# A decoder step on one core: a new order for the mixing stage, the output projection in eight pieces

## The reference, cut to what matters

```
u = rmsnorm(x, norm_mix) @ w_in                    # split into the head groups
m = concat(swa(q, k, v, sinks), gated_deltanet(conv(c), z, a, b, S0, ...))
h = x + m @ w_out
hn = rmsnorm(h, norm_ffn)
y = h + hierarchical_moe(hn, w_router_group, w_router_expert, ...)   # top 1 group, top 2 experts in it
out = rmsnorm(y, norm_final)
# gated delta rule, block by block, state S carried along:
#   v_new = u - w @ S;  o = q_dec @ S + qk @ v_new;  S = S * g_tot + k_dec.T @ v_new
# where u, w come from the inverse of (I + strictly lower (k k^T * beta * decay))
```

## Time and profile before

| | |
|---|---|
| median of 3 runs | 2366.58 us (2365.85 to 2373.49) |
| the profiled execution | 2381.16 us, its span 2379.3 us |
| mean granted clock of PE over the span | 0.949 |
| PE busy | 2218.0 us, 93% |
| DVE / ACT / POOL busy | 1276.8 / 543.3 / 641.1 us |
| positions start at | 0: 753.84, 1: 794.73, 2: 839.91, 5: 976.00, 6: 1047.45, 8: 1137.52, 11: 1280.29, 14: 1421.98, 15: 1471.21, 16: 1523.81 us |

### The profile page before, as it was taken

How to read it: one execution, slowest core, us unless ns; L and a number is a source line. 1 busy time by engine, 2 the same in 40 slices (tenths; PEclk the granted TensorE clock), 3 DMA queues, 4 the chain that set the end, 5 groups by cost and what they waited for, 6 DMA issues and landing times. The chain is left out here.

```text
span 2379.3 us, 47036 instructions
## 1 busy us (share of the span) xinstructions
PE 2218.0 (93%) x18536; PEld 1208.7 (51%) x18536; DVE 1276.8 (54%) x2659; ACT 543.3 (23%) x1417; POOL 641.1 (27%) x819
## 2 busy tenths in 40 slices
PE   7999999999976999899999999857999999999977
PEld 4454454454444666666666666633444444444433
DVE  4514325232424565355665746436776677667746
ACT  3202103112112343233434333310000000000013
POOL 1020100100200110211132231315655555555552
PEclk9999999999986899889999989977999999999998
DMA  8041040130168031112311221137999999999957
GB/s 310 18 136 47 24 142 23 47 112 13 35 180 219 6 118 53 51 57 87 108 62 62 97 87 62 44 146 276 351 366 366 367 374 367 376 377 372 351 224 311
DMA packets 171951, 405.87 MB, mean 171 GB/s; under 512 B 51187, under 2 KB 92771, under 8 KB 147161
## 3 DMA queue, kind: packets, MB, share of 16 engines
q1 hardware_dynamic: 142423, 350.39, 41.3%
q0 software_dynamic: 23648, 35.19, 4.1%
q10 hardware_dynamic: 5698, 17.67, 1.9%
HBM read 344.98 MB, written 94.80 MB: 185 GB/s over the span
## 5 line engine op out<-in xcount | busy, mean ns | idle before, releaser
L876 PE MATMUL p_ps<-p_xt,p_w 128*128 128x512 f32 x1088 | 474.1, 594 | 0.5 <-DVE p_xt L697 0.5
L3075 PE MATMUL p_ps<-p_w_arena,p_x_arena 128*128 128x512 f32 x1024 | 452.4, 595 | 11.1 <-DVE p_x_arena L2977 11.1
L876 PEld LDWEIGHTS p_ps<-p_xt,p_w 128*128 128x128 f32 x1088 | 204.1, 190 | 253.7 <-issue 248.5
L3075 PEld LDWEIGHTS p_ps<-p_w_arena,p_x_arena 128*128 128x128 f32 x1024 | 195.4, 191 | 257.4 <-issue 246.1
L2731 POOL DMA_INDIRECT p_x_arena<-s_hn,p_slot x272 | 276.8, 1018 | 122.2 <-issue 85.7
L2371 PE MATMUL p_ps<-p_w_out,p_mixt 128*128 128x512 f32 x544 | 258.5, 620 | 0.2 <-DVE p_mixt L1977 0.2
L2999 DVE STREAM_TRANSPOSE p_y_arena<-p_y_arena 32x64 f32<-32x64 f32 x1024 | 241.0, 235 | 13.2
L3084 PE MATMUL p_ps<-p_w_arena,p_y_arena 128*128 128x512 f32 x512 | 230.2, 592 | 3.2 <-DVE p_y_arena L2999 3.2
L3084 PEld LDWEIGHTS p_ps<-p_w_arena,p_y_arena 128*128 128x128 f32 x512 | 97.2, 190 | 126.0 <-issue 126.0
L2371 PEld LDWEIGHTS p_ps<-p_w_out,p_mixt 128*128 128x128 f32 x544 | 101.7, 197 | 107.6 <-issue 104.3
L885 PE MATMUL p_ps<-p_w,p_xt 128*128 128x144 f32 (+1 forms) x512 | 146.6, 439 | 0.0
(11 more groups left out here) (419 smaller groups left out, 2852.1 us busy)
## 6 DMA issues: line engine op xcount, KB each, us to landing
p_w_arena<-in_w_exp_gate SPq DMA_DIRECT2D x64, 1024.0 KB
p_w_arena<-in_w_exp_up SPq DMA_DIRECT2D x64, 1024.0 KB
p_w_arena<-in_w_exp_down SPq DMA_DIRECT2D x64, 1024.0 KB
p_w_arena<-s_y SPq DMA_DIRECT2D x16, 1024.0 KB, 14.7
p_x<-in_x_prompt SPq DMA_DIRECT2D x30, 512.0 KB, 4.8
p_w<-in_w_in SPq DMA_DIRECT2D x4, 2048.0 KB
p_spread<-s_roots SPq DMA_DIRECT2D x16, 512.0 KB, 7.0
s_kv<-p_us SPq DMA_DIRECT2D x32, 256.0 KB
```

The source lines that it names most:

```text
L876: ins = mm(ps[:, job % 4, :], w[:, c, at:at + P], xt[s % 2][:, c, :], start=(c == 0), stop=(c == KC - 1))
L3075: t = mm(ps[:, 2 + b, :], xt[b][:, c, :], w_gu[bw][:, :, c, :], start=(c == 0), stop=(c == KC - 1))
```

## The change

- PE's `project` takes pieces of two chunks. Eight pieces are spread over the whole position t for tile t - 1, the last at its end; so `layer_sum(t - 2, 1)` comes first in the next position, and `layer_norm`, `turn_hn` and `logits` follow in position t for tile t - 2. `mixt` and `h` become two buffers each.
- `pair_sums` go to banks 2 and 3 (behind `query_keys` of the tile before), `turn_hn` to banks 2 and 3, `logits` to bank 2, the count to bank 3 as a call of its own (`counts`) in positions 10, 13 and 16. `key_products` waits for `dec_ready`.
- DVE: `score_experts` and `pick_group` go one position later, to 9, 12 and 15, among the rounds of the inverse; `shift_logits` and `count_experts` to the position's end; `output_norm` ahead of `window_output`; in position 5 both masks ahead of `state_terms`.
- ACT: `layer_square(t - 2)` first; `spread_inverse` ahead of `far_copy` with its corner (`spread_corner`) behind it; `pair_decays(t + 2)` last.
- POOL: `layer_root(t - 2)` first, ahead of `spread_gates(t + 2)`; `send_rows` last.
- SP: the window ahead of x, and x of tile t - 2 in the round of tile t.
- Ahead of the loop: `pair_sums(0)` before the wait for the exponentials, `pair_sums(1)` and `pair_decays(1)` earlier, `ident` loaded with the first constants.

The diff below follows SP, POOL, ACT, DVE and PE in this order; PE's new functions stand ahead of its loop.

```diff
-        load_x(t - 1)
         load_window(t)
+        if t > 2:
+            load_x(t - 2)
+    load_x(NQ - 2)
     load_x(NQ - 1)
...
     for t in range(NQ):
         if t == 1:
             own_gates()
+        if t > 1:
+            layer_root(t - 2)
         if t + 2 < NQ:
             spread_gates(t + 2)
         if t in PLACE_AT:
             weigh_rows(PLACE_AT[t])
             place_rows(PLACE_AT[t])
-        if t in SEND_AT:
-            send_rows(*SEND_AT[t])
         if t == SI:
             sample_states()
         output_roots(t)
         if t + 1 < NQ:
             key_decay(t + 1)
-        if t:
-            layer_root(t - 1)
+        if t in SEND_AT:
+            send_rows(*SEND_AT[t])
+    layer_root(NQ - 2)
     layer_root(NQ - 1)
...
+
+    def spread_corner(t):
+        b = t % 2
         x_done.after(act, t)
...
     for t in range(NQ):
-        front, back = t + 1 < NQ, t > 0
+        front, back, far = t + 1 < NQ, t > 0, t > 1
+        if far:
+            layer_square(t - 2)
         if t == SI:
             sample_products()
         if back:
             turned_mix(t - 1)
         gate_tanh(t)
         first_values(t)
+        if t in PLACE_AT:
+            counts(PLACE_AT[t])
         probabilities(t)
         new_values(t)
+        if far:
+            turned_hn(t - 2)
         normalize(t)
+        output_squares(t)
+        turned_probabilities(t, 0)
+        if far:
+            logits(t - 2)
+        turned_probabilities(t, 2)
+        if front:
+            spread_inverse(t + 1)
+            far_copy(t + 1)
+            spread_corner(t + 1)
+        if t + 2 < NQ:
+            pair_decays(t + 2)
         if t in GROUP_AT:
             exponents(GROUP_AT[t])
-        output_squares(t)
-        turned_probabilities(t, 0)
-        turned_probabilities(t, 2)
-        if back:
-            layer_square(t - 1)
-        if t + 2 < NQ:
-            pair_decays(t + 2)
-        if back and front:
-            turned_hn(t - 1)
-        if front:
-            far_copy(t + 1)
-        if back and front:
-            logits(t - 1)
-        if front:
-            spread_inverse(t + 1)
     turned_mix(NQ - 1)
+    layer_square(NQ - 2)
...
-        front, back = t + 1 < NQ, t > 0
-        state_terms(t)
-        mask(t, 0)
-        if front:
+        front, back, far = t + 1 < NQ, t > 0, t > 1
+        if far:
+            layer_sum(t - 2, 1)
+        if t == SI:
+            mask(t, 0)
+            mask(t, 1)
+            state_terms(t)
             lower(t + 1)
-        mask(t, 1)
+        else:
+            state_terms(t)
+            mask(t, 0)
+            if front:
+                lower(t + 1)
+            mask(t, 1)
         if front:
             query_keys(t + 1)
         maxima(t)
...
             causal(t + 1)
             first_inverse(t + 1)
         second_values(t)
+        if far:
+            layer_norm(t - 2)
         if front:
             level_products(t + 1, 0)
         if back:
             layer_sum(t - 1, 0)
         output_gate(t)
         denominators(t)
...
-        if t in EXPERTS_AT:
-            picks[EXPERTS_AT[t]].pick_first()
+        if far:
+            turned_hn(t - 2)
         if front:
             level_update(t + 1, 0)
         state_update(t)
...
             level_products(t + 1, 1)
         if t == SI:
             sample_update(1)
+        output_squares(t)
+        if front:
+            level_update(t + 1, 1)
         turned_probabilities(t, 1)
         if front:
-            level_update(t + 1, 1)
-        output_squares(t)
+            level_products(t + 1, 2)
+        if t in EXPERTS_AT:
+            dve.wait_ge(on["exps"], EXPERTS_AT[t] + 1)
+            picks[EXPERTS_AT[t]].pick_group()
+        if front:
+            level_update(t + 1, 2)
+        if t == SI:
+            sample_update(2)
+        if t in EXPERTS_AT:
+            picks[EXPERTS_AT[t]].score_experts()
+        if front:
+            level_products(t + 1, 3)
+        turned_probabilities(t, 3)
+        if front:
+            level_update(t + 1, 3)
+        output_norm(t)
+        if t == SI:
+            sample_update(3)
+        if t in EXPERTS_AT:
+            picks[EXPERTS_AT[t]].pick_first()
+        window_output(t)
         if t in GROUP_AT:
-            dve.wait_ge(on["exps"], GROUP_AT[t] + 1)
-            picks[GROUP_AT[t]].pick_group()
-        if front:
-            level_products(t + 1, 2)
-        turned_probabilities(t, 3)
+            shift_logits(GROUP_AT[t])
         if t in EXPERTS_AT:
             count_experts(EXPERTS_AT[t])
-        if t == SI:
-            sample_update(2)
-        if not front:
-            output_norm(t)
-        if back:
-            layer_sum(t - 1, 1)
-        if front:
-            level_update(t + 1, 2)
-        window_output(t)
-        if front:
-            level_products(t + 1, 3)
-        if t == SI:
-            sample_update(3)
-        if back:
-            layer_norm(t - 1)
-        if front:
-            level_update(t + 1, 3)
-        if back and front:
-            turned_hn(t - 1)
-        if front:
-            output_norm(t)
-        if t in GROUP_AT:
-            picks[GROUP_AT[t]].score_experts()
         if t == 0:
             dve.wait_ge(on["weights_in"], WEIGHTS_IN)
             nc.vector.tensor_scalar(w_out[:, 4:8, :], w_out[:, 4:8, :], gain_o[:], 0.5, ALU.mult, ALU.mult
                                     ).then_inc(on["weights_scaled"], 1)
+    layer_sum(NQ - 2, 1)
+    layer_norm(NQ - 2)
     layer_sum(NQ - 1, 0)
...
     def pair_sums(t):
+        qk_read.after(pe, t - 1)
+        lt_ready.after(pe, t - 1)
+        lg_ready.after(pe, t - 4)
         gt_ready.after(pe, t)
...
     def key_products(t):
         b = t % 2
         pe.wait_ge(kq_in[b], use(t))
         invt_ready.after(pe, t - 1)
+        dec_ready.after(pe, t)
...
-            dec_ready.after(pe, min(t + 1, NQ - 1))
-            lg_ready.after(pe, t - 2)
+            h_ready.after(pe, t - 2)
+            swa_mixed.after(pe, t - 1)
...
+    def project(t, piece):
+        n, first = piece // 4, 2 * (piece % 4)
+        if piece == 0:
             swa_mixed.after(pe, t)
-            if n:
-                mixt_act.after(pe, t)
-        else:
+        elif piece == 2:
             mixt_act.after(pe, t)
-        for c in range(4 * part, 4 * part + 4):
-            ins = mm(ps[:, 7 - n, :], mixt[:, c, :], w_out[:, c, n * 512:(n + 1) * 512],
+        for c in (first, first + 1):
+            ins = mm(ps[:, 7 - n, :], mixt[t % 2][:, c, :], w_out[:, c, n * 512:(n + 1) * 512],
                      start=(c == 0), stop=(c == KC - 1))
-        if part:
+        if piece % 4 == 3:
             ins.then_inc(proj_done.sem, 1)
...
+    def counts(t):
+        pe.wait_ge(on["both_ready"], PLACE_AT[t] + 1)
+        qk_read.after(pe, min(t + 1, NQ - 1))
+        lt_ready.after(pe, min(t + 1, NQ - 1))
+        earlier(mm, ps[:, 3, :], choices[PLACE_AT[t]], upto, ones).then_inc(on["counts_done"], 1)
...
+    pair_sums(0)
     pe.wait_ge(on["e_ready"], 3)
-    pair_sums(0)
     key_products(0)
     pe.wait_ge(on["second_in"], SECOND_IN)
     diagonal_blocks(0)
+    pair_sums(1)
...
-    dec_ready.after(pe, 0)
-    pair_sums(1)
...
     for t in range(NQ):
-        front, back = t + 1 < NQ, t > 0
+        front, back, far = t + 1 < NQ, t > 0, t > 1
         state_products(t)
         scores(t, 0)
         if front:
...
             pe.wait_ge(on["weights_in"], WEIGHTS_IN)
             pe.wait_ge(on["weights_scaled"], 1)
         if back:
-            project(t - 1, 0, 0)
+            project(t - 1, 0)
+            project(t - 1, 1)
         new_values(t, 0)
         if back:
-            project(t - 1, 0, 1)
+            project(t - 1, 2)
+        if t in PLACE_AT:
+            counts(t)
         if front:
             diagonal_blocks(t + 1)
         new_values(t, 1)
+        if back:
+            project(t - 1, 3)
         if front:
             level_products(t + 1, 0)
         new_values(t, 2)
-        if back:
-            project(t - 1, 1, 0)
+        if far:
+            turn_hn(t - 2)
         if front:
             level_update(t + 1, 0)
         state_and_output(t)
         if front:
             level_products(t + 1, 1)
-        turn_probabilities(t, 0)
-        turn_probabilities(t, 1)
+        if back:
+            project(t - 1, 4)
         if front:
             level_update(t + 1, 1)
         if t == SI:
             sample_kdv(1)
-        turn_probabilities(t, 2)
-        turn_probabilities(t, 3)
+        turn_probabilities(t, 0)
+        turn_probabilities(t, 1)
         if front:
             level_products(t + 1, 2)
-        if back:
-            project(t - 1, 1, 1)
+        if far:
+            logits(t - 2)
         if front:
             level_update(t + 1, 2)
         if t == SI:
             sample_kdv(2)
+        if back:
+            project(t - 1, 5)
+        if front:
+            level_products(t + 1, 3)
+        turn_probabilities(t, 2)
```

(77 more changed lines are left out.)

83 lines of the change are left out of this document (36 added, 47 removed).

## The result

The new kernel takes 2343.7 us (median of four runs, 2339.15 to 2346.47) against 2366.2 (four runs, 2363.89 to 2373.49): ratio 0.990, 95% interval 0.987 to 0.992. So it is 22.5 us faster, about 1%, inside the range 2304 to 2356, and 20 us above the 2324 forecast.

What follows compares the result with a forecast made beforehand. PE, busy 93% of the span, was taken as the bound, with at most 73.7 us to win. Terms -16.0 + 1 + 3.3 - 9 - 25 + 3 = -42.7 took 2366.6 to 2324 us; range 2304 to 2356.

Steps and rivals of the forecast that it cites:

- the shared port: DVE's state subtraction and scaling against POOL's spread_gates early in each position: +3 us taken, bounds 0 and 18.
- rival (b): The DVE and POOL port collision is met in all fourteen positions: 18 us in place of 3, 2339; chance 0.12.
- Waits for DVE, -16.0 + 1: PE's 16.0 us of waits for DVE in positions 1 to 15 go, 1 us kept in position 5.
- The choices, +3.3: score_experts delays DVE ahead of level_products 3 in positions 9, 12, 15; PE waits 1.1 us three times.
- Issue stalls, -9: PE's 13.7 us of stalls no semaphore explains, positions 1 to 15: 9 go as the load burst becomes parts.
- Clock, -25: PE's lower clock in positions 1 to 15: 25 us won, bounds 0 and -44, as projection pieces break light stretches.
- Head and tail, 0: Ahead of and behind the loop: moved pair_sums +2.3 to -2.3, row sends under projection halves; both taken as 0.
- key_products and dec: key_products now waits for ACT's late dec_ready; covered by the last piece and state_products, cost 0, 0.8 us spare.
- Rival (a): The clock and issue stalls stay, as the loads meet another light stretch: 2355 to 2358, say 2356; chance 0.17.
- rival (d): Slower: the load at each position's start stalls PE and drops its clock there: +116 us, 2409; chance 0.06.
- near 58: Sign in the new profile that the forecast is right: position 5, which took 71.45 us, is near 58.
- the undisturbed position: Sign that the forecast is right: a position without disturbance takes 43 to 43.9 us, 44.32 less 0.45.

Runs made afterwards that it cites:

- gates_first: The new kernel with two POOL calls exchanged, spread_gates ahead of layer_root again; 2324.5 us, ratio 0.981 to the kernel before.
- pieces_paired: gates_first with projection piece 3 directly behind piece 2 and piece 4 together with piece 5, piece 7 left; 2353.2 us, ratio 0.997.
- x_first: The new kernel with the load of x ahead of the window's load again, all loads in one burst; 2343.8 us, ratio 0.990.
- burst_late: gates_first with loads of window, keys and values held back until the previous position's first probabilities are turned; 2334.4 us, ratio 0.988.
- second profile of before: The kernel before, unchanged, profiled a second time; this execution took 2357.9 us.
- tail_only: gates_first with one POOL edit: the six row sends of the last position go behind layer_root(15); 2317.0 us, ratio 0.979.
- piece7_early: gates_first with projection piece 7 directly behind piece 6, ahead of window_output; 2328.7 us, ratio 0.985.
- tail_picks: gates_first with the last position's row sends behind layer_root(15) on POOL and score_experts behind level_update 3 on DVE; 2326.1 us, ratio 0.984.
- pieces_merged: The new kernel with projection piece 3 behind piece 2, 4 with 5, and 7 with 6 ahead of window_output; 2361.1 us, ratio 0.998.

## Why the prediction was right in direction and 20 us off

**The step that failed** is the shared port: "I lean to DVE", and +3. It is a term that was mis-sized, by which of two instructions starts first. POOL started 0.4 us ahead and the term was 20.9 in twelve positions; rival (b), which said just this, had a chance of 0.12, and its 2339 is the nearest of the times given. The upper bound of 18 was a little low, since a position's wait is up to 1.74 and I took 1.3, which was what PE waited in position 5, behind other cover. gates_first shows the term alone: 18 to 19 us, and 2324.5 us without it. That this is the forecast's own time is in part luck, since other terms were off both ways and nearly cancel (below). The Trainium skill ("SBUF — State Buffer", "Who interferes with whom") says that of such a pair the one that starts first blocks the other; it doesn't say which one that will be. The trace agrees in both directions: the scaling behind `spread_gates` takes 2.12 us in place of 0.42, and `spread_gates` behind the subtraction 2.24 in place of 1.90.

**Waits for DVE, -16.0 + 1.** Nearly right: 2.9 us are left beside the choices and the port (0.7, 0.5, 0.4, one of 0.3, and two of 0.5 at `level_update` in positions 1 and 5). pieces_paired shows that the pieces are the cover: 6.7 us at new_values as soon as piece 3 moves. That piece 3 and 4 also cover level_update and turn_hn, 8 us more, the prediction had not seen.

**The choices, +3.3.** Right in sum: of the 4.1 in five waits theirs are 1.29, 1.29 and 0.48 in positions 9, 12 and 15, 3.1 together. Position 15 pays less than the 1.1 that was priced for each.

**Issue stalls, -9.** The size was low: of 15.3 (the prediction counted 13.7), 1.3 are left, -14.0. The reason was half right. The burst was hardly split, and drawing it together again did nothing (x_first); its place had a part: it lies some 4 us into the position now and not over the small products of the tail (burst_late, 8.8 us of stalls again). The other part is the pieces between the rows of small products (pieces_paired, 7.6 us again). Each of the two alone brings back about half, so how the 14 us divide between them isn't shown.

**Clock, -25.** In the profiled executions 44 us became 0.06 x 58.6 = 3.5, all in position 5, so -40. But against the second profile of before it is 28 to 3.5, -25. PE's busy time in positions 1 to 15 says it more finely: 695.0 and 676.2 us in the two profiles of before, 654.8 after, of which about 4 us is work that now stands in position 16. That leaves 36 and 17 us for the clock, and, as the median of before (2366.2) lies between the two executions (2381.2 and 2357.9), an estimate of 24 for the median. The term was priced on an execution with more falls than usual, and the sum then carried to the median; the caution (-25 of -44) made up for that. It was right for the median by luck more than by reason.

**Head and tail, 0.** Head right (position 1 starts at 793.50 against 794.73). From the start of position 16 to the end it is +8.7 us. About 4 of these are moved work (`turn_hn` and `logits` of tile 14, 3.0, and a count, 1.2), which the prediction rightly priced at net 0, since positions 1 and 15 lose it. The other 4.5 or so the prediction did not have. In the tail `turn_hn(15)` waits 2.53 us for the root behind the six row sends, which the prediction had named and covered with two halves of a projection; 2.5 in place of 0. tail_only takes it away. The last 2 us lie in the expert stage: from its first row of 128 x 512 products to the end it takes 754.7 us in place of 752.2. No run looked for the reason.

**key_products and dec**, cost 0: right, 0.3 us once, but only by piece 7 (piece7_early, 0.3 us in twelve). Rival (a), clock and stalls stay, and rival (d), stalls at the head, fell: both the new kernel and x_first have full DMA engines from 4 us into each position, at no cost. Of the other signs that the prediction named, position 5 came out as said (58.60 for "near 58"), and the undisturbed position took 44.7 for 43 to 43.9, which is the port.

What the 20 us are, together, each as measured less forecast: port +17.9, tail about +4.5, waits for DVE +1.9, clock about +1, the choices -0.2, head -1.2, issue -5.0; that makes 19 of the 19.8 us, with two of the terms estimated. Open: what PE waits for in an issue stall, and which of the stalls bring the clock down. Most stalls come at fixed products of PE's list (the two profiles of before, above). It may be that a burst costs nothing where no such place lies under it; no run tested that. In position 5 of the new kernel, gates_first and tail_only the clock first falls (near 971, 963 and 962) with PE busy in all of the 6 us ahead of it.

## What to carry to other kernels

When two engines share a port and their instructions start within some tenths of a microsecond, price the collision at its full length in every round, and give the order on the engine with slack so that the long instruction starts somewhere else; here two exchanged calls gave 18 to 19 us, nearly as much again as the whole rewrite. Put large matrix products between rows of small ones: here they covered the other engines' short operations, and with them went most of PE's stalls. Try a burst of loads beside large products and not beside rows of small ones. When work is moved past the end of a loop, look at the stretch behind the loop as well; here it gave back 8.7 of 46 us. And profile the kernel before twice ahead of pricing its clock.

## What the runs showed of the hardware that was not expected

- A small DVE operation with two operands in SBUF waits as long as a large one: an addition for the choice of experts, 0.20 us otherwise, took 1.75 us in tail_picks beside `spread_gates`. The reduction ahead of it, with one operand, overlapped with `spread_gates` (the last line), and neither of the two was lengthened by it:

```profile
1184.58 0.20 DVE L2014 TENSOR_REDUCE p_vc<-p_vc 128x5 f32<-128x40 f32 x1
1184.81 1.75 DVE L1108 TENSOR_TENSOR p_vc<-p_vc 128x40 f32<-128x40 f32 x1
1184.60 1.90 POOL L1442 TENSOR_TENSOR p_gt<-p_gates,p_upto 128x1024 f32<-128x1024 f32 x1 [13.18 <-PE p_ps L2152]
```

- PE's issue stalls come with a burst of loads and without one. Seven loads within six microseconds cost nothing over `key_products`, `turn_mix` and the first pieces (x_first); six within four microseconds were followed by stalls of up to 2.3 us in rows of 64 products of 32 x 32 (burst_late). With the DMA share below 0.1, such rows and `logits` stalled for up to 1.4 us (pieces_merged). `state_products` is no safe place either: in the kernel before it stalled for 0.9 us at a share of 1.06 (position 9).
- The same program, the kernel before, took 2356 to 2383 us from run to run, and in its two profiles positions 1 to 15 took 729.08 and 708.85 us at nearly the same waits: 18.8 of the 20.2 us are PE's busy time on the same products, at 0.94 and 0.96 of the clock.
